# Neighbourhood attention: probabilities turned unscaled, the output made by query and turned to features afterwards

## What is computed

```python
def neighbourhood_attention(z, q_g, k_g, rpb):
    ...
    q = split(rmsnorm(z[..., :D].reshape(B, L, H, dh), q_g) * (dh ** -0.5))
    k = split(rmsnorm(z[..., D:2 * D].reshape(B, L, H, dh), k_g))
    v = split(z[..., 2 * D:])
    ...
    def row_block(i):
        ...
        s = jnp.einsum('bhqd,bhrqwd->bhqrw', q_i, k_win).astype(jnp.float32)
        ...
        s = s + jnp.transpose(bias, (0, 2, 1, 3)).astype(jnp.float32)[None]
        pr = jax.nn.softmax(s.reshape(B, H, GRID_W, kh * kw), axis=-1).reshape(B, H, GRID_W, kh, kw)
        return jnp.einsum('bhqrw,bhrqwd->bhqd', pr.astype(v.dtype), v_win)
```

## Time and profile before

| | |
|---|---|
| time, median of 3 runs | 3614.68 us (3613.87 to 3616.26) |
| span of the profiled execution | 3620.0 us |
| last vector instruction of the profiled execution starts | 3615.37 us |
| the attention stage in it, first score to last copy | 3083.49 to 3150.46 us |
| TensorE / VectorE / ScalarE busy over the span | 93% / 50% / 31% |
| TensorE / VectorE / ScalarE busy, 3084 to 3151 us | 60.56 / 53.63 / 51.30 of 67.00 us |

### The profile page before, as it was taken

The page is one execution under the profiler, slowest core; times in us unless marked ns, Lnnn a source line. Parts: engine busy times, 40 slices in busy tenths (PEclk is TensorE's granted clock), DMA queues, the critical chain, the costliest instruction groups (busy, mean ns, idle before and its releaser), DMA issues. The chain is left out here.

```text
span 3620.0 us, 55834 instructions
## 1 busy us (share of the span) xinstructions
PE 3349.8 (93%) x23830; PEld 2339.7 (65%) x23830; DVE 1812.7 (50%) x2866; ACT 1112.7 (31%) x1877; POOL 252.8 (7%) x210
## 2 busy tenths in 40 slices
PE   8889889998988987999989788889999999899999
PEld 7587533332667753333258688857888878588887
DVE  3755433322466443333244766566665462766635
ACT  3543300000345330000032333224433432743423
POOL 1011000000101100000020222201000110010001
PEclk9999899999989998999999899999999999999999
DMA  5031279999402217999952000012222222122222
GB/s 220 13 117 70 110 321 428 428 427 427 194 36 96 91 59 323 428 428 427 427 201 105 2 3 3 3 36 99 93 93 88 99 93 82 64 94 93 93 86 78
DMA packets 54389, 595.58 MB, mean 165 GB/s; under 512 B 5760, under 2 KB 10112, under 8 KB 16512
## 3 DMA queue, kind: packets, MB, share of 16 engines
q1 hardware_dynamic: 54144, 592.03, 40.6%
HBM read 589.91 MB, written 2.10 MB: 164 GB/s over the span
## 5 line engine op out<-in xcount | busy, mean ns | idle before, releaser
L681 PE MATMUL psum<-source_hi,weights_hi 128*128 128x512 f32 (+1 forms) x2352 | 920.6, 391 | 47.0 <-DVE weights_lo L568 39.0
L681 PE MATMUL psum<-source_hi,weights_lo 128*128 128x512 f32 (+1 forms) x2352 | 910.3, 387 | 0.0
L681 PE MATMUL psum<-source_lo,weights_hi 128*128 128x512 f32 (+1 forms) x2352 | 910.3, 387 | 0.0
L681 PEld LDWEIGHTS psum<-source_hi,weights_hi 128*128 128x128 f32 x2352 | 447.7, 190 | 145.7 <-DVE weights_lo L568 45.7
L681 PEld LDWEIGHTS psum<-source_lo,weights_hi 128*128 128x128 f32 x2352 | 448.3, 191 | 89.6 <-issue 2.9
L681 PEld LDWEIGHTS psum<-source_hi,weights_lo 128*128 128x128 f32 x2352 | 447.5, 190 | 88.6
L516 ACT CAST weights_hi<-weight_ring 128x1024 fp32r<-128x1024 f32 (+4 forms) x304 | 289.6, 960 | 661.5 <-PE psum L681 650.4
L568 DVE TENSOR_TENSOR weights_lo<-weight_ring,weights_hi 128x1024 fp32r<-128x1024 f32 (+4 forms) x304 | 340.7, 1126 | 301.4 <-ACT weights_hi L516 300.7
L1767 DVE TENSOR_TENSOR x<-psum,x 128x512 f32<-128x512 f32 x250 | 160.5, 685 | 207.2 <-PE psum L1614 207.2
L630 POOL TENSOR_TENSOR sums_of_squares<-squares 128x512 f32<-128x512 f32 (+1 forms) x17 | 27.2, 1600 | 2509.0 <-ACT squares L536 2509.0
L1578 PE MATMUL psum<-lent_weights,branches 128*64 128x512 f32 x800 | 182.1, 597 | 3.6 <-DMA lent_weights<-in_w_gate 2.5
(11 more groups left out here) (388 smaller groups left out, 4557.6 us busy)
## 6 DMA issues: line engine op xcount, KB each, us to landing
lent_weights<-in_w_down SPq DMA_DIRECT2D x26, 2048.0 KB, 18.9
lent_weights<-in_w_up SPq DMA_DIRECT2D x24, 2048.0 KB, 20.7
lent_weights<-in_w_gate SPq DMA_DIRECT2D x22, 2048.0 KB, 19.5
weight_ring<-in_ffn_w_up SPq DMA_DIRECT2D x22, 2048.0 KB, 7.7
weight_ring_first<-in_w_gate SPq DMA_DIRECT2D x18, 2048.0 KB, 17.3
weight_ring_first<-in_w_up SPq DMA_DIRECT2D x18, 2048.0 KB, 19.3
weight_ring<-in_w_gate SPq DMA_DIRECT2D x18, 2048.0 KB, 17.1
weight_ring<-in_w_up SPq DMA_DIRECT2D x18, 2048.0 KB, 19.6
```

The lines of the kernel that those rows point to most:

```text
L681: ins = pe.matmul(ps, a, b, start=k == 0 and q == 0, stop=k == job.rows // P - 1 and q == 2)
```

## The change

Three things change, all in `near_attention`.

- VectorE no longer scales the probabilities. `turn(j)` waits for the exponentials themselves (`exp_done`).
- `out(j)` exchanges the operands: the turned probabilities (128 keys by 128 queries) are now stationary and the values (64 features) move, so that the result lies by query, 128 queries by two heads of 64 features, in the first 128 columns of bank 6. The same number of matmuls is issued. A new VectorE function `scale_rows(j)` multiplies this tile by the reciprocals on its way to SBUF (`rows_out`).
- A new TensorE function `turn_out(j)` turns the scaled tile to features, into bank 7, one transpose a step. `keep(p)` reads bank 7, which no longer takes turns with another bank: `turn_out` of a pair's first step waits for `out_kept` of the pair before.

TensorE's loop at step `j` is now `score(j + 2)`, `turn(j)`, `turn_out(j - 2)`, `out(j - 1)`; VectorE's is `row_max(j + 2)`, `keep` at `j % 4 == 2`, `scale_rows(j - 1)`.

```diff
@@ TensorE
                 for a in range(2):
-                    pe.wait_ge(prob_ready, 2 * j + a + 1)
+                    pe.wait_ge(exp_done, 2 * j + a + 1)
...
             def out(j):
                 p, qt = divmod(j, TT)
                 pe.wait_ge(turned_kept, j + 1)
-                if p >= 2 and qt == 0:
-                    pe.wait_ge(out_kept, p - 1)
-                for s, tile in enumerate(key_tiles(qt)):
-                    for a in range(2):
-                        ins = pe.matmul(K.psum[rows(a), 6 + p % 2, qt * P:(qt + 1) * P],
-                                        v[:, tile, (2 * p + a) * HEAD:(2 * p + a + 1) * HEAD],
-                                        probT[:, p % 2, qt, a, s, :], start=s == 0, stop=s == 1)
-                if qt == TT - 1:
-                    ins.then_inc(out_ready, 1)
+                if j:
+                    pe.wait_ge(rows_kept, j)
+                for a in range(2):
+                    for s, tile in enumerate(key_tiles(qt)):
+                        ins = pe.matmul(K.psum[:, 6, rows(a)], probT[:, p % 2, qt, a, s, :],
+                                        v[:, tile, (2 * p + a) * HEAD:(2 * p + a + 1) * HEAD], start=s == 0, stop=s == 1)
+                ins.then_inc(out_ready, 1)
+
+            def turn_out(j):
+                p, qt = divmod(j, TT)
+                pe.wait_ge(rows_kept, j + 1)
+                if p and qt == 0:
+                    pe.wait_ge(out_kept, p)
+                pe.transpose(K.psum[:, 7, qt * P:(qt + 1) * P], rows_out[:, j % 2, :], K.ident).then_inc(out_turned, 1)
...
                 turn(j)
+                if j >= 2:
+                    turn_out(j - 2)
                 if j:
                     out(j - 1)
+            turn_out(n - 2)
             out(n - 1)
+            turn_out(n - 1)
@@ VectorE
             def keep(p):
-                dve.wait_ge(out_ready, p + 1)
-                src = K.psum[:, 6 + p % 2, :].rearrange("p (c r) -> p c r", c=GRID_W)
+                dve.wait_ge(out_turned, TT * (p + 1))
+                src = K.psum[:, 7, :].rearrange("p (c r) -> p c r", c=GRID_W)
...
+            def scale_rows(j):
+                b = j % 4
+                dve.wait_ge(exp_done, 2 * (j + 1))
+                link(dve.reciprocal(st[:, b, INV], st[:, b, SUM]))
+                dve.wait_ge(out_ready, j + 1)
+                if j >= 2:
+                    dve.wait_ge(out_turned, j - 1)
+                dve.tensor_tensor(rows_out[:, j % 2, :].rearrange("p (a d) -> p a d", a=2),
+                                  K.psum[:, 6, 0:P].rearrange("p (a d) -> p a d", a=2),
+                                  st[:, b, INV].unsqueeze(2).to_broadcast([P, 2, HEAD]), ALU.mult).then_inc(rows_kept, 1)
+
             row_max(0)
             row_max(1)
             for j in range(n):
-                b = j % 4
-                dve.wait_ge(exp_done, 2 * (j + 1))
-                link(dve.reciprocal(st[:, b, INV], st[:, b, SUM]))
-                for a in range(2):
-                    dve.tensor_scalar(prob[:, b, a, :], prob[:, b, a, :], st[:, b, 4 + a:5 + a], None, ALU.mult)\
-                        .then_inc(prob_ready, 1)
                 if j + 2 < n:
                     row_max(j + 2)
                 if j % TT == 2 and j // TT >= 1:
                     keep(j // TT - 1)
+                if j:
+                    scale_rows(j - 1)
+            scale_rows(n - 1)
             keep(pairs - 1)
@@ ScalarE, copy(j)
-                if p >= 2 and qt == 0:
-                    act.wait_ge(out_ready, p - 1)
+                if j >= 2 * TT:
+                    act.wait_ge(out_ready, j - 2 * TT + 1)
```

More of the change, by code:

```diff
@@ L2960, in near_attention @@
         st = K.sbuf(ctx, "softmax_stats", [P, 4, 6])
-        block, (scores, dlink, biased, exp_done, prob_ready, turned, turned_kept, out_ready, out_kept) = ctx.enter_context(
-            stage(nc, "scores_ready", "dve_link", "scores_biased", "exp_done", "probs_ready", "probs_turned", "turned_kept",
-                  "output_ready", "output_kept"))
+        rows_out = K.sbuf(ctx, "output_rows", [P, 2, P])
+        block, (scores, dlink, biased, exp_done, turned, turned_kept, out_ready, rows_kept, out_turned, out_kept) = \
+            ctx.enter_context(stage(nc, "scores_ready", "dve_link", "scores_biased", "exp_done", "probs_turned", "turned_kept",
+                                    "output_ready", "output_rows_kept", "output_turned", "output_kept"))
         SUM, INV = (slice(2 * i, 2 * i + 2) for i in (1, 2))
```

## The result

The kernel after took 3676.03 us, median of six runs, against 3614.68. The ratio on record, estimated from all runs and not the quotient of the two medians (1.0170), is 1.0138, 95% interval 1.0115 to 1.0160. The median hides the main thing. The kernel before had six runs within 2.4 us; the changed one had two at 3645.5 and 3645.9, one at 3670.3 and three from 3681.8 to 3682.9, and the longer the run, the lower its mean granted clock: 0.965, 0.964, 0.956, and 0.951 to 0.954. The profiled execution is the 3645.5 one.

A forecast was written before the change was run, and what follows sets the result against it. TensorE was taken to bound ordinary steps, VectorE only the `keep` step. Terms 17.9 (seven pairs) + 1.3 (start) + 2.1 (end) - 0.8 - 0.3 = +20.2 us on 3614.7 gave 3635 us; 8-in-10 range 3622 to 3648.

The forecast's parts named there:

- what bounds the stage: Attention stage: TensorE bounds ordinary steps at 1.80 us; VectorE's scaling is hidden by 0.4 us.
- the keep step: One step in four, where VectorE is the bound: 0.6 us per pair, 4 us in all for lighter VectorE work.
- the output group: Output matmuls with operands exchanged: weight loads bind, 0.112 us each, eight in 0.89 us where it was 0.42.
- Rival 1: Output matmuls stream at 0.055 us a record, loads fully hidden: 14 us less, 3621 us; chance 0.09.
- the change of shape: Between TensorE's groups: about 0.17 us of gap where array use changes; one of three such changes goes.
- rival 2: TensorE's groups show more first loads or only partly overlap load and stream: up to +11, 3646 us; chance 0.12.
- the stall at bank 7: A pair's first `turn_out` waits for `keep`: TensorE stands still 1.48 us, in seven pairs.
- Rival 4: The wait for `keep` is mostly covered because `keep` gets through earlier: 10 us less, 3625 us; chance 0.04.
- The sum: All terms of the attention stage together: +20.2 us, giving 3635 us, +0.56%, with a stage about 87 us long.
- the baseline: Whole kernel: the difference, worked out inside an execution spanning 3620.0 us, was added to the median of 3614.68.
- rival 3: The clock falls in the stalls, slowing two steps in each of seven pairs: +20, 3655 us; chance 0.05.
- One of my own signs of being wrong: Middle of the attention stage: a granted clock below 1 there would show the forecast wrong.

The follow-up runs named there:

- the filler kernel: The changed kernel with three unread matmuls (1.3 us) on TensorE in the stall before the wait for `keep`: 3634.2 us, ratio 1.0041.
- the second set: Runs sharing one chip, with the unedited changed kernel (3643.9 us, ratio 1.0074) and three altered kernels beside the kernel before (3620.5 us).
- one bank: The kernel before with its output in one PSUM bank only and `keep` one step earlier: 3621.1 us, ratio 1.0014.
- full stream: The changed kernel with each output matmul streaming both heads' values, 128 columns for 64, the unwanted half unread: 3636.0 us, ratio 1.0053.
- the first set: The changed kernel against the kernel before, six runs: 3676.03 us against 3614.68, ratio 1.0138.

## Why the prediction was wrong

**Right: what bounds the stage.** TensorE sets the ordinary step; taking VectorE's scaling away altogether gave 6 us, with 4 read from the keep step.

**Right: the output group.** 0.112 us a record, eight in 0.89, was taken from loads with one moving column; measured are about 0.11 each. Doubling the streamed columns added 0.05 us a step. Rival 1 is out.

**Right: the change of shape.** The gaps between the three whole-array groups are gone; a step is 2.16 to 2.17 for 2.22, so rival 2 is out too.

**Right: the stall at bank 7.** 2.62 us from score to `turn_out` for 2.61, seven times. Moving `keep` by one step took it away and shortened the stage at full clock from 82.6 us (the filler kernel's) to 72.6, 10.0 us for 7 x 1.48 = 10.4. Rival 4 is out.

**The sum, nearly.** The stage of the first profile is 86.1 us, for "about 87", with two stretches at half clock in it; at full clock it would be some 83. The forecast time was too low by some 8 us more, for the baseline that the sum was added to.

**Wrong: the clock.** The step that failed is rival 3: chance 0.05, price "two steps in each of seven pairs: +20, 3655 us", dismissed because "the middle of the stage has idle time at every `keep` and a granted clock of 1.00". That row was true of the kernel before and I carried it over to another load. The idle time there is 0.5 us a time:

```profile
PE psum L2993 <- DVE probs L3049: 4.3, 9, 0.5
```

Afterwards it is 1.3, and the steps between are different too. One of my own signs of being wrong, a granted clock below 1 in the stage's middle, is met in all five traces of the changed kernel. The price had the wrong form as well. I took half clock as something that each stall costs and that ends, as it did at the start of the stage before. In the changed kernel's traces one stall of seven brings it on in mid-stage, and it lasts 3.4 us or to the end of the stage: 1.84 us a step, 59 us if all 32 steps were slow (an estimate). Runs of 3670 to 3685 lie within that; my range ended at 3648. The median of the second set, 3643.9, lies inside my range; that is luck, since the trace of that set shows the long stretch.

**What brings the clock down.** The experiments leave a combination:

| | no stall | stall, idle | stall, filled |
|---|---|---|---|
| output as before | before: 3609.7 to 3625.7 | one bank: 3616.6 to 3629.6 | |
| output with 64 columns per load | `keep` earlier: 3619.1 to 3632.0 | **after: 3640.1 to 3685.2** | filler: 3629.1 to 3634.9 |
| output with 128 columns per load | | full stream: 3633.7 to 3646.1 | |

Only the cell in bold shows half clock in mid-stage, in all of its five traces, long in two, and runs beyond 3650 in 10 of 18. With each of three changes in one respect (idle time away, idle time filled, array streaming through the loads) the clock is 1.00 in every trace of the stage, four in all, and none of 30 runs is above 3646.1.

The three don't weigh the same. Without the stall there are twenty runs and two traces, and with the stall filled four runs and one trace, on a chip where the changed kernel had three of four above 3657: so it is shown that the idle time is needed. That the output group with 64 columns per load is needed too rests on less: six runs and one trace with 128 columns, on a chip where the changed kernel itself had only two of six above 3650, and the kernel with one bank, which differs in its whole output path. And all these traces begin with an early first score and a full clock; what the altered kernels do behind a late start wasn't seen. Why the two together do it, and why one execution falls behind the first stall and another behind the fourth, stays open.

**Where the 61 us of the first set went.** About 19 are the forecast mechanism at full clock: some 83 us of stage against 64 to 65, which is the 66.9 of before less the 2 to 3 us that its own half clock at the start cost (estimates). The rest, some 40 us, goes with the clock, as the runs' clocks say. How much of it lies in the stage and how much ahead of it (up to 12 us, by the starts of the first score) isn't shown, for there is no trace of a run that long.

## What to carry to other kernels

Price both operands of a matmul: here the fp32 load of 128 columns was the cost, 0.11 us a record, with 1 and with 64 moving columns, and 128 added next to nothing. When an engine isn't the bound, taking work off it gives only what the one step gives in which it is (here 6 us for 18.5 us less of busy time), so look at what the rearrangement asks of the engine that is. And a new idle stretch in TensorE's loop must be priced at both clocks: ask whether the loop would keep the clock with the stretch in it, and if that isn't sure, move the wait (one line here, 21 us in the median of the second set) or fill it.

## What the runs showed of the hardware

- With TensorE busy 26.27 of 28 us by its records, the granted clock stayed at half for over 50 us, and came back 4 us into the next stage's dense matmuls. The busy share in the profile didn't tell whether the clock would return.
- The kernel with the least busy TensorE (58.6 of 71 us, one output bank) held the full clock, and the busier one (74.8 of 87) didn't.
- In five traces of the changed kernel the granted clock fell 1.2 to 2.2 us behind the end of an idle stretch of 1.3 us, and in seven traces of the altered kernels it stayed at 1.00 through the stage, in two of them with seven such stretches (one output bank, 128 columns streamed).
- Adding work made the kernel faster: 1.3 us of filler per pair (3634.2 for 3662.8). With twice the streamed columns (3636.0 for 3643.9) the intervals of the ratios just overlap.
- In the kernel before 0.17 us without a load stands where the whole array gives way to 64 columns (ahead of the output) and 64 columns to 64 rows (ahead of the score). Between groups that all use the whole array none does, even with a semaphore wait between that is already met, and from the whole array to 64 rows it is 0.06 us.
